# Two of a unit's 28 weight-split subtractions move from VectorE to GpSimd

## What is computed

```python
for l in range(DEPTH):                      # 2
    h = rmsnorm(x, norm_w[l])               # (1, 256, 2048), float32
    proj = einsum('bld,dn->bln', h, w_in[l])
    y_a = gdn_branch(...);  y_b = hgrn2_branch(...)
    y_c = s5_branch(...);   y_d = retention_branch(...)
    branch = einsum('blcw,cwd->blcd', stack([y_a, y_b, y_c, y_d]), w_branch[l])
    merged = sum(sigmoid(gate_logits) * branch, axis=2)
    x = x + einsum('bld,de->ble', merged, w_out[l])
return rmsnorm(x, final_norm_w)
```

## Time and profile before

| what | value |
|---|---|
| device time, median of 3 executions | 2991.35 us (2990.71 to 2993.51) |
| span of the profiled execution | 2988.6 us |
| TensorE matmul busy | 2916.0 us, 98% |
| VectorE busy | 2073.8 us, 69% |
| ScalarE busy | 1489.5 us, 50% |
| GpSimd busy | 340.3 us, 11% |
| weight subtractions on VectorE (L1118) | 912, 1227 ns each |
| granted TensorE clock, mean | 0.998 of full speed |

### The profile page before, as it was taken

How to read it: one execution, slowest core, us unless ns; L and a number is a source line. 1 busy time by engine, 2 the same in 40 slices (tenths; PEclk the granted TensorE clock), 3 DMA queues, 4 the chain that set the end, 5 groups by cost and what they waited for, 6 DMA issues and landing times.

```text
span 2988.6 us, 49428 instructions
## 1 busy us (share of the span) xinstructions
PE 2916.0 (98%) x19452; PEld 2662.7 (89%) x19452; DVE 2073.8 (69%) x3417; ACT 1489.5 (50%) x2209; POOL 340.3 (11%) x525
## 2 busy tenths in 40 slices
PE   7999999999999999999999999999999999999998
PEld 7899999999998888888899999999999988888887
DVE  7887788778776555545568877787788755555555
ACT  6445545554554444444555455545555644444443
POOL 3112022212200000000010221122120000000000
PEclk9999999999999999999999999999999999999999
DMA  6455555555556666665645555555555566666655
GB/s 171 125 148 152 147 141 152 148 146 145 152 161 192 194 193 193 194 193 182 196 112 142 146 152 152 145 143 152 143 144 150 176 193 195 191 196 190 196 178 168
DMA packets 614104, 492.34 MB, mean 165 GB/s; under 512 B 18545, under 2 KB 496561, under 8 KB 613489
## 3 DMA queue, kind: packets, MB, share of 16 engines
q1 hardware_dynamic: 606800, 483.44, 54.5%
q0 software_dynamic: 6688, 4.64, 0.8%
q10 hardware_dynamic: 384, 1.11, 0.1%
HBM read 487.02 MB, written 2.10 MB: 164 GB/s over the span
## 4 chain that ended last, share of the span: by engine, by line
PE 56%; issue 24%; DVE 14%; DVEq 5%; ACT 1%; DMA 0%; POOL 0%; ACTq 0%; POOLq 0%
PE PJ L1702 35%; PE S L1702 7%; PE HA L1702 4%; PE GA L1702 4%; PE RA L1702 3%; DVE w_lo L1118 3%; PE GB L1702 2%; DVE region L1281 2%; DVEq L1256 2%; DVE region L1289 1%; DVE mix L1229 1%; DVEq L1306 1%; DVE work L1252 1%; DVEq L1321 1%; DVE work L1241 1%
## 5 line engine op out<-in xcount | busy, mean ns | idle before, releaser
L1118 DVE TENSOR_TENSOR w_lo<-raw_w,w_hi 128x1024 fp32r<-128x1024 f32 x912 | 1117.9, 1227 | 715.8 <-ACT w_hi L573 693.5
L573 ACT ACTIVATE w_hi<-raw_w 128x1024 fp32r<-128x1024 f32 x912 | 962.5, 1058 | 780.1 <-PE PJ L1702 324.7
L1702 PE MATMUL PJ<-h_hi,w_hi 128*128 128x256 f32 x3584 | 1046.3, 292 | 0.0
L1702 PE MATMUL PJ<-h_hi,w_lo 128*128 128x256 f32 x3584 | 1014.1, 283 | 0.0
L1702 PE MATMUL PJ<-h_lo,w_hi 128*128 128x256 f32 x3584 | 1013.9, 283 | 0.0
L1702 PEld LDWEIGHTS PJ<-h_hi,w_hi 128*128 128x128 f32 x3584 | 686.4, 192 | 12.9 <-issue 12.6
L1702 PEld LDWEIGHTS PJ<-h_lo,w_hi 128*128 128x128 f32 x3584 | 686.8, 192 | 0.0
L1702 PEld LDWEIGHTS PJ<-h_hi,w_lo 128*128 128x128 f32 x3584 | 685.8, 191 | 0.0
L1702 PE MATMUL PJ<-w_hi,h_hi 128*128 128x512 f32 x640 | 249.2, 389 | 1.9 <-DVE h_lo L1611 1.9
L1702 PE MATMUL PJ<-w_lo,h_hi 128*128 128x512 f32 x640 | 249.0, 389 | 0.0
L1702 PE MATMUL PJ<-w_hi,h_lo 128*128 128x512 f32 x640 | 249.0, 389 | 0.0
(11 more groups left out here) (427 smaller groups left out, 4156.8 us busy)
## 6 DMA issues: line engine op xcount, KB each, us to landing
raw_w<-w_in SPq DMA_DIRECT2D x704, 512.0 KB, 3.6
raw_w<-w_branch SPq DMA_DIRECT2D x128, 512.0 KB, 4.4
raw_w<-w_out SPq DMA_DIRECT2D x64, 512.0 KB, 3.6
raw_w<-s_glu_w SPq DMA_DIRECT2D x16, 512.0 KB, 5.3
ret_decay<-c_ret POOLq DMA_DIRECT2D x16, 128.0 KB, 3.0
out<-x_tok SPq DMA_DIRECT2D x4, 512.0 KB, 4.0
x_tok<-x SPq DMA_DIRECT2D x1, 1024.0 KB, 7.7
x_tok<-x ACTq DMA_DIRECT2D x1, 1024.0 KB, 8.3
```

The lines of the kernel that those rows point to most:

```text
L573: A_(w_hi[i % RING][:, :, :], raw_w[i % RING][:, :, :], ACT.Copy).then_inc(hi_ready, 1)
L1118: TT(w_lo[i % RING][:, :, :], raw_w[i % RING][:, :, :], w_hi[i % RING][:, :, :].bitcast(f32), ALU.subtract).then_inc(raw_used[i % RING], 1)
L1702: return nc.tensor.matmul(o, w, m, start=start, stop=stop)
```

## The change

GpSimd makes the low parts of pieces 18 and 22 of every unit, right behind the S5 matrices of the next unit and ahead of the HGRN norm. VectorE leaves these two out. TensorE's, ScalarE's and SP's lists stay as they are: `raw_used` is incremented once per piece, now by GpSimd for these two, and GpSimd waits for `hi_ready` as VectorE did.

```diff
+POOL_LOW = (18, 22)
...
                     if n1 < DEPTH * UNITS:
                         s5_matrices(n1)

+                    for i in POOL_LOW:
+                        pool.wait_ge(hi_ready, l * SPLITS + u * HALVES + (i + 1))
+                        nc.gpsimd.tensor_tensor(
+                            w_lo[i % RING][:, :, :], raw_w[i % RING][:, :, :], w_hi[i % RING][:, :, :].bitcast(f32),
+                            ALU.subtract).then_inc(raw_used[i % RING], 1)
+
                     def inverse_root(ms):
...
                     def ahead(i):

-                        split_lo(i + RING, s0)
+                        if i + RING not in POOL_LOW:
+                            split_lo(i + RING, s0)
```

## The result

The changed kernel takes 3012.79 us (median of 4 runs, 3009.45 to 3014.13) against 2991.03 us, a ratio of 1.0068 with a 95% interval of 1.0056 to 1.0081: 21.8 us slower. The forecast was 3012.5 us.

A forecast was written before the change was run, and what follows sets the result against it. TensorE, 98% busy, bounds the kernel through its waits for VectorE. 17.1 us from 14 usual units and 4.1 from two first ones make +21.2 on 2988.6; with the median's 2.75 us, 3012.5 us, range 2986 to 3031.

The forecast's parts named there:

- TensorE's wait is the only thing to gain: TensorE, busy 98% of the span: only its waits can be gained; any longer wait is lost in full.
- Removing piece 22 is worth 1.13 us, removing piece 18 nothing: VectorE's list before the rotated k, usual units; in each layer's first unit piece 18 is worth 1.13 us too.
- The length on GpSimd: One GpSimd subtraction of 1024 elements takes 2.3 us, extended from 256 elements at 2.1 ns per further element.
- the prediction's other estimate, 2.2 us: GpSimd subtraction of 1024 elements, from the reference page's 2.6 cycles per element at 1.2 GHz.
- The norm is not late: GpSimd's HGRN norm: even at 3 us each the two subtractions end some 9 us before it.
- a longer latency costs nothing: Pieces and buffers ready later on GpSimd cost zero; some 6 us more in each would change that.
- The hold of 2.15 us: A VectorE operation with two SBUF inputs waits 2.1 ns per element behind GpSimd's: 2.15 us for 1024.
- The sign that L1312 would be long: Profile after: the VectorE operation behind piece 21's subtraction takes about 2.4 us instead of 0.28, once per unit.
- A PSUM reader is not held up: VectorE operations reading PSUM run through GpSimd's at piece 18; the following two-input one loses 0.2 us.
- The wait changes place: TensorE's wait at the rotated k falls from 1.03 to about 0.3 us; the HGRN step's becomes about 1.9 us.
- The sum: Whole kernel: +1.22 us in each of 14 usual units, 2.04 us in each of two first units, together +21.2 us.
- rival 1: VectorE gets in between GpSimd's long operation, so only the saving is left: -16.5 us, 2974.9 us; chance 0.17.

The follow-up runs named there:

- extra: The kernel before plus one 1024-element GpSimd subtraction that nothing reads, at piece 22's moment in 14 of 16 units, VectorE's list whole: 3021.59 us, ratio 1.0099.
- only22: The changed kernel, but GpSimd makes piece 22 alone and VectorE makes piece 18 as before: 3007.19 us, 1.0051 of the kernel before.
- extra1: As extra, on the kernel before, but the added GpSimd operation is a copy of 1024 elements with one input: 3001.98 us, ratio 1.0037.
- only18: The changed kernel, but GpSimd makes piece 18 alone and VectorE makes piece 22 as before: 2994.41 us, 1.0009 of the kernel before.
- tiny: The changed kernel, but GpSimd subtracts only 8 of the 1024 elements of pieces 18 and 22: 2968.39 us, 0.9922 of the kernel before.
- half: The changed kernel, but GpSimd subtracts only 512 of the 1024 elements of pieces 18 and 22: 2986.14 us, 0.9984 of the kernel before.
- later22: The kernel before with VectorE's subtraction of piece 22 moved behind the rotated k, GpSimd as before: 2974.35 us, ratio 0.9944.

## Why the prediction was right, point by point

- **TensorE's wait is the only thing to gain, and a longer wait is lost in full.** Right. With the waits taken at the weight loads, which come ahead of the matmuls, those for the two VectorE places grew from 41.4 us to 61.6 us: +20.2 us of the 21.8. Before:

```profile
PEld HA L1702 <- DVEq L1321: 21.5, 23, 2.2
PEld RA L1702 <- DVEq L1509: 19.9, 16, 1.4
```

  The same sum follows the time in most other runs: extra +30.0 us (time +30.8), only22 +15.9 (+15.9), extra1 +11.7 (+11.2), only18 +3.8 (+3.1), tiny -20.8 (-22.9). half and later22 are taken up below.
- **Removing piece 22 is worth 1.13 us, removing piece 18 nothing.** Right for the units that are not a layer's first. In the changed kernel VectorE waits 1.69 us for the product in GA at piece 18's old place, and L1260 begins 0.65 us behind the start of that product, as before.
- **The length on GpSimd, 2.3 us.** 2.37 to 2.39 us where it is undisturbed, 2.81 with its wait for the turn; the prediction's other estimate, 2.2 us, was 0.2 us short. The norm is not late: GpSimd still waits 10.5 us for `h_ms_ready` in unit 3. That a longer latency costs nothing held too: nothing waits for line 527.
- **The hold of 2.15 us, extended from operations of 64 and 128 elements to 1024.** This was the one large risk. 2.18 us measured, with 1.10 us at 512 elements on the same line. The Trainium skill's exclusive lock (page "SBUF — State Buffer", section "Who interferes with whom") is borne out here at 1024 elements. The sign that L1312 would be long once per unit held in 14 units; in the two others the hold was there on other instructions.
- **A PSUM reader is not held up.** L1260 kept its 0.49 us for two, while GpSimd's operation ran from 414.12 to 416.51. L1312 behind it lost 0.17 us (forecast 0.2).
- **The wait changes place**, from 1.03 to 0.3 us at the rotated k and about 1.9 us at the HGRN step. Right: 1.74 us measured at the HGRN step in unit 3, and at the rotated k 4.4 us in 16 waits, 0.28 us each, at the weight load.
- **The sum.** The starts of the retention scores (RA<-rx) in the traces, in us, show where the time goes:

| kernel | unit 0 | unit 7 | unit 8, first of layer 2 | unit 15 |
|---|---|---|---|---|
| before | 119.41 | 836.80 | 1598.62 | 2314.26 |
| changed | 124.05 | 849.07 | 1613.20 | 2336.99 |
| tiny | 116.83 | 825.28 | 1585.08 | 2292.22 |

  The changed kernel is 4.64 us late in unit 0 and 22.73 us late in the last unit. 2.72 us of both are not the change's: the profiled execution was that much late at a product in unit 0 that comes ahead of piece 18, with the same wait in front of it:

```profile
88.78 0.49 PE L1702 MATMUL HA<-hkq,work 128*128 128x128 f32 x2 [1.98 <-DVEq L1321]
91.50 0.49 PE L1710 MATMUL HA<-hkq,work 128*128 128x128 f32 x2 [1.98 <-DVEq L1329]
```

  1.17 us of it were there at a product some 22 us earlier (68.26 against 67.09). The rest came with a lower TensorE clock: from 60 to 70 and from 70 to 80 us the mean granted clock was 0.93 and 0.90 of full speed, where the trace of before has 1.00, and from 69.5 to 71.5 us the matmuls PJ<-h_lo,w_hi took 0.41 us in place of 0.28.

  So in the trace the change costs 20.0 us where 21.2 were forecast. By the differences of the two upper rows of the table, the 14 usual units cost 15.8 us, 1.13 each (forecast 1.22), and the first units of the layers 1.9 and 2.3 us (forecast 2.04 each; the second number includes the stretch between the layers). The median's agreement to 0.3 us is partly luck.

One term was mis-sized, in **rival 1**, which did not come true: without a hold the gain is 22.9 us (tiny), not 16.5. The wait had been priced by the matmul's idle time, 1.03 us. TensorE loses more: its weight load waits too, 19.9 us in 16 waits or 1.24 us each. In tiny each of the 14 usual units is 1.25 us shorter, 17.4 us in all. The two first units, 2.6 and 2.0 us shorter, give the rest of the trace's 22.0: there both subtractions lay in VectorE's chain (2 x 1.13 = 2.26 us), as the prediction says, but rival 1's price had left piece 18 out.

later22 got 16.4 us although its two waits fell by more, from 41.4 to 21.9 us. The retention scores of its unit 3 begin 3.67 us earlier than before (422.46 against 426.13), the transposes of the retention values a few us behind them only 3.48 us (427.40 against 430.88): 0.2 us per unit is given back in between, at a wait that before does not have. What ends it, the trace does not show ("issue"):

```profile
PEld RA L1962 <- issue: 3.1, 16, 0.2
```

The time of half was 5.1 us under before where 0 to 1 was expected. Its trace agrees with the theory: the two waits sum to 41.2 us, as before (41.4), and the span is 2987.7 us, 0.9 us under that of before. But its profiled execution took 2989.5 us, 3.4 us more than its median, so the trace does not show what made the others faster. The interval of the timed runs, -2 to -7 us, does not quite reach the forecast, and that rest stays open.

## What to carry to other kernels

Work given to GpSimd is not off VectorE's path when it reads SBUF while VectorE runs instructions with two SBUF inputs: such an instruction stood still for the whole body of GpSimd's, here 2.18 us to save 1.13 us. Look at what VectorE runs in that very stretch, not at whether GpSimd has a gap. In these runs GpSimd did no harm where VectorE waited or read PSUM, but where VectorE waits nothing is gained either. Before moving work to another engine, see whether it can stand a few instructions later on its own: that took the same wait away for 0.2 us per unit.

## What the runs showed of the hardware

- The hold by size, two inputs on GpSimd, two SBUF inputs on VectorE: 0.13 us at 64 elements, 0.26 at 128, 1.10 at 512 (half), 2.18 at 1024 (changed kernel), so 2.0 to 2.15 ns per element throughout. With one input on GpSimd (a copy, extra1) 0.85 us at 1024. Whichever had begun first held up the other: GpSimd the VectorE subtraction in unit 0, VectorE's subtraction GpSimd in unit 3 (2.81 us in place of 2.39).
- GpSimd alone: 2.39 us for 1024 elements with two inputs against VectorE's 1.22 us. The copy took at least 1.04 us.
- The idle time in front of a matmul understates a wait; the one in front of its weight load was 0.2 us longer here and is the nearer measure of what can be won back (1.25 us per unit in tiny).
